# Stick-breaking attention: q out of PSUM ahead of v and weights, turned weights copied ahead of the second sigmoids

## What is computed

```python
def block(args):
    i, q_i = args
    q_pos = i * Q_BLOCK + jnp.arange(Q_BLOCK)          # Q_BLOCK = 128
    z = jnp.einsum('bhqd,bhkd->bhqk', q_i, k).astype(jnp.float32) * scale
    mask = key_pos[None, :] < q_pos[:, None]
    log_beta = jax.nn.log_sigmoid(z)
    log_one_minus = jnp.where(mask, jax.nn.log_sigmoid(-z), 0.0)
    later = lax.cumsum(log_one_minus, axis=3, reverse=True) - log_one_minus
    weights = jnp.where(mask, jnp.exp(log_beta + later), 0.0)
    return jnp.einsum('bhqk,bhkd->bhqd', weights.astype(v.dtype), v)
```

## Time and profile before

| | |
|---|---|
| median of 3 runs | 1345.59 us (1342.94 to 1350.71) |
| the profiled execution | 1345.15 us, span 1343.6 us |
| TensorE busy | 1222.4 us, 91% of the span |
| VectorE busy | 902.5 us, 67% |
| ScalarE busy | 741.0 us, 55% |
| GpSimd busy | 305.6 us, 23% |

### The profile page before, as it was taken

One profiled execution on the slowest core, in us unless ns is written; L12 is line 12 of the kernel. 1 busy time (PEld: TensorE's weight loads), 2 busy tenths in 40 slices (PEclk: granted clock), 3 DMA queues, 4 the chain that ended last, 5 costly groups with the idle time before them and its releaser, 6 DMA issues. The chain is left out here.

```text
span 1343.6 us, 18137 instructions
## 1 busy us (share of the span) xinstructions
PE 1222.4 (91%) x6596; PEld 957.9 (71%) x6596; DVE 902.5 (67%) x847; ACT 741.0 (55%) x758; POOL 305.6 (23%) x270
## 2 busy tenths in 40 slices
PE   3999999999899988599937999999999999999975
PEld 2778776877688767388825777777777777777742
DVE  4256565655466258334576989898898888988825
ACT  6155555554352233312234787777777877777713
POOL 0000000000211001000051444444444444444400
PEclk9999999999899995599967999999999999999988
DMA  5210101000211020173328999999999999999747
GB/s 172 63 32 17 32 17 31 18 17 1 64 32 32 1 94 32 45 244 109 111 97 292 408 387 383 382 382 386 384 384 375 381 377 385 374 391 389 293 175 296
DMA packets 85840, 271.63 MB, mean 202 GB/s; under 512 B 14640, under 2 KB 48544, under 8 KB 61216
## 3 DMA queue, kind: packets, MB, share of 16 engines
q1 hardware_dynamic: 75760, 249.89, 50.2%
q0 software_dynamic: 8880, 16.87, 3.8%
q10 hardware_dynamic: 1152, 4.19, 0.8%
HBM read 253.91 MB, written 25.79 MB: 208 GB/s over the span
## 5 line engine op out<-in xcount | busy, mean ns | idle before, releaser
L1886 PE MATMUL ps<-w_high,x_hi 128*128 128x512 f32 x512 | 206.3, 403 | 4.8 <-DVE hid L1812 2.9
L1886 PE MATMUL ps<-w_lower,x_hi 128*128 128x512 f32 x512 | 203.5, 397 | 0.0
L1886 PE MATMUL ps<-w_high,x_lo 128*128 128x512 f32 x512 | 203.4, 397 | 0.0
L1153 POOL DMA_INDIRECT x_g<-h_dram,who x33 | 160.2, 4854 | 40.2 <-POOL who L1149 27.6
L1826 DVE TENSOR_TENSOR d_lo<-cat,d_hi 128x2048 fp32r<-128x2048 f32 x64 | 146.3, 2287 | 25.5 <-ACT d_hi L1747 25.5
L1798 DVE TENSOR_TENSOR w_lower<-w_raw,w_high 128x2048 fp32r<-128x2048 f32 x62 | 141.7, 2286 | 24.7 <-ACT w_high L1726 24.7
L1803 DVE TENSOR_TENSOR w_lower<-w_raw,w_high 128x2048 fp32r<-128x2048 f32 x64 | 143.4, 2279 | 0.0
L1732 ACT ACTIVATE w_high<-w_raw 128x2048 fp32r<-128x2048 f32 x62 | 118.8, 1917 | 25.5 <-PE ps L1886 25.5
L1747 ACT ACTIVATE d_hi<-cat 128x2048 fp32r<-128x2048 f32 x64 | 122.2, 1910 | 17.0 <-PEq L1233 13.5
L1726 ACT ACTIVATE w_high<-w_raw 128x2048 fp32r<-128x2048 f32 x62 | 118.3, 1908 | 0.0
L1886 PEld LDWEIGHTS ps<-w_high,x_hi 128*128 128x128 f32 x512 | 97.0, 189 | 28.5 <-DVE w_lower L1798 3.3
(11 more groups left out here) (276 smaller groups left out, 2401.0 us busy)
## 6 DMA issues: line engine op xcount, KB each, us to landing
w_raw<-exp_w_gate SPq DMA_DIRECT2D x64, 1024.0 KB, 7.0
w_raw<-exp_w_up SPq DMA_DIRECT2D x64, 1024.0 KB, 9.0
cat<-exp_w_down SPq DMA_DIRECT2D x64, 1024.0 KB, 8.0
w_raw<-w_in SPq DMA_DIRECT2D x25, 512.0 KB, 3.9
xt<-x SPq DMA_DIRECT2D x8, 512.0 KB, 7.6
w_raw<-w_out SPq DMA_DIRECT2D x8, 512.0 KB, 5.3
x_g<-x SPq DMA_DIRECT2D x8, 512.0 KB, 3.8
x_dram<-cat SPq DMA_DIRECT2D x8, 512.0 KB, 4.9
```

The source lines that it names most:

```text
L1153: pool.indirect_dma_start(x_g[0:CAP, j, :], None, k["h2_dram"][:, :], bass.IndirectOffsetOnAxis(ap=who[j][0:CAP, 0:1], axis=0), bounds_che ...
L1886: mm = pe.matmul(out, x_[:, n // 3, :], w_[:, n // 3, :], start=(n == 0), stop=(n == 3 * KD - 1))
```

## The change

It has two parts. In step 0 of each pair, `evict` and `evict_lo` of the group that ends there (q's first half) stand ahead of `copy_v` and the split, on ScalarE and on VectorE; in all other steps they stay where they were. And `sigmoids` is cut in two, `scan_sigmoids` and `weight_sigmoids`: in steps 3 to 6 of each pair `copy_w(g-1)` stands between the two, in the other steps behind both, as before. Nothing is added or left out: each engine has as many instructions as before.

```diff
+    copies_first = (3, 4, 5, 6)
...
-            def sigmoids(g):
+            def scan_sigmoids(g):
                 b = g % 2
                 if g >= 2:
                     act.wait_ge(scan_done, 2 * g - 2)
...
                     act.activation(stay[:, b, :, s:e], ps[:, 2 * (c % 2):2 * (c % 2) + 2, 0:e - s], ACT.Sigmoid,
                                    scale=-SCALE).then_inc(stay_done, 1)
+
+            def weight_sigmoids(g):
+                b = g % 2
                 if g >= 2:
                     act.wait_ge(turned, turns[g - 2] + len(parts(g - 2)))
                 for n, (s, e) in enumerate(chunks(g)):
...
                 if g < STEPS:
-                    sigmoids(g)
+                    scan_sigmoids(g)
+                    if n not in copies_first:
+                        weight_sigmoids(g)
                 if g >= 1:
                     copy_w(g - 1)
+                if g < STEPS and n in copies_first:
+                    weight_sigmoids(g)
+                ends = p < SB_PAIRS and 24 in (part[1] for part in fill[n] if part)
+                if ends and n == 0:
+                    evict(6 * (p + 1) + group_at[n])
                 if g < STEPS and n == 0:
                     copy_v(p)
                 if g < STEPS and n in split_at and 3 * p + split_at[n] < TILES:
                     split_hi(3 * p + split_at[n])
-                if p < SB_PAIRS and 24 in (part[1] for part in fill[n] if part):
+                if ends and n:
                     evict(6 * (p + 1) + group_at[n])
...
                 if g < STEPS:
                     weights(g)
-                    if n in split_at and 3 * p + split_at[n] < TILES:
-                        split_lo(3 * p + split_at[n])
-                if p + 1 < SB_PAIRS and group_at[n] < 4 and 24 in (part[1] for part in fill[n] if part):
+                lows_out = p + 1 < SB_PAIRS and group_at[n] < 4 and 24 in (part[1] for part in fill[n] if part)
+                if lows_out and n == 0:
+                    evict_lo(6 * (p + 1) + group_at[n])
+                if g < STEPS and n in split_at and 3 * p + split_at[n] < TILES:
+                    split_lo(3 * p + split_at[n])
+                if lows_out and n:
                     evict_lo(6 * (p + 1) + group_at[n])
                 if g >= 1:
                     evict_o(g - 1)
```

## The result

The changed kernel takes 1332.83 us (median of 4 runs, 1331.71 to 1333.32), the kernel before 1344.41 us (median of 4, 1342.94 to 1350.71; a fourth run of 1343.23 us joined the three shown ahead of the prediction). The ratio is 0.9906 with a 95% interval of 0.9877 to 0.9935: faster by 0.9%, clear of no change. Forecast were 1336.7 us, with a range of 1332 to 1342, and a gain of 8.5; the median moved by 11.6, and the time lies at the low end of the range. The profiled executions differ by about as much: span 1343.6 before, 1331.5 now.

What follows compares the result with a forecast made beforehand. TensorE, busy 91% of the span, was taken as the bound, so only its waits and slow clock could be won. The terms -9.4 + 2.1 - 1.2 = -8.5 us took 1345.15 to 1336.7 us, range 1332 to 1342.

Steps and rivals of the forecast that it cites:

- The bound and the mechanism of q: TensorE, 91% busy, bounds; early q removes step 1's three 1.91 us waits for `q_lo` and the slow clock behind.
- -9.4: Step 1 of all pairs: 6.2 us of waits and 3.2 us of slow clock in pairs 1 and 2 go.
- The copies in the first three pairs: Steps 3 to 6: late second sigmoids delay `k_lo`, costing 0.7 us a pair, +2.1 us in all.
- The copies in the last pair: Steps 3 and 4: nothing waits for low parts, so gaps of 0.89 and 0.31 us are won, -1.2 us.
- All later work follows it unchanged, so this goes to the end: Behind the stage: its closing barrier passes the summed gain of 8.5 us unchanged to the end of the run.
- One: Step 4: the new 1.3 us wait for `k_lo` pulls the clock down, 1338.3 to 1341.5 us; chance 0.26.
- Two: Step 1: the clock's falls stay or come back later, hanging on something besides the gap, 1339.9 us; chance 0.13.
- Three: First three pairs: `k_lo` doesn't bind, so the copies win 0.89 us each, 1331.9 us; chance 0.08.
- Four: Steps 3 and 5: ScalarE reloads its table when switching between copy and sigmoid, +15.4 us, 1352.1 us; chance 0.03.
- the bound of 1338.9: Whole run: a time under it, a change of 0.5% or 6.7 us, counts as faster.

Runs made afterwards that it cites:

- experiment 1: The changed kernel with only q let out first in step 0, no copies moved: 1331.62 us, ratio 0.9899.
- experiment 6: The kernel before the change, with ScalarE splitting the weight tile of step 0 twice for a longer gap: 1357.38 us, ratio 1.0065.
- Experiment 2: The changed kernel with only the copies moved, q back behind the copies of v and the split: 1342.20 us, ratio 0.9979.
- experiment 3: The changed kernel with copies first in steps 3 and 4 only, no longer in 5 and 6: 1333.15 us, ratio 0.9906.
- experiment 4: The changed kernel with copies first in the last pair only: 1331.82 us, ratio 0.9883.
- experiment 5: The kernel of experiment 3, with VectorE making `k_lo` ahead of the multiplication in step 3: 1333.22 us, ratio 0.9887.

## Why the prediction was right or wrong

**The bound and the mechanism of q** were right. The wait for `q_lo` and the slow clock behind it are both gone in all pairs; experiment 1 has the whole gain of the stage from this part alone, and experiment 6 shows that a longer gap brings half clock in every pair. The term "-9.4" was mis-sized: it measured -10.4 (9.94 + 11.53 + 11.57 + 8.49 less 31.12). Its clock part, 3.2 us, came as forecast; the waits gave 7.2 instead of 6.2. I took the gap as the profile's idle time, 1.91 us. That is counted from the modelled end of the turning, and a matmul that follows at once starts before that end (at 143.48, where the turning ends at 143.10 + 0.63 = 143.73). From start to start the place shrank by 2.53 - 0.38 = 2.15 us, 0.24 more than the idle time, and about as much more in each of the four pairs.

**The copies in the first three pairs** were right to 0.2 us. Forecast: a wait of 1.3 us for `k_lo` in step 4, 0.5 in step 6, 0.7 us lost a pair. Measured: 1.48, 0.53 and 0.65. Experiment 2 gives the same with q last, in experiment 3 the wait and the loss of step 6 go alone, in experiment 4 both waits, and 5 shows which order on VectorE makes the wait.

**The copies in the last pair** were mis-sized the same way: -1.2 from the idle times, -1.8 measured, 1.64 of it in steps 3 and 4, where the records say 0.89 and 0.31 and the starts 1.10 and 0.54. The two parts together: +2.1 - 1.2 forecast, +0.2 measured.

**"All later work follows it unchanged, so this goes to the end"** is the step that failed for the whole run. It put what happens behind the stage at nothing, and the runs showed 1.3 us of gain there in the median (11.6 less 10.25) and 1.8 in the span. Of the 3.1 us by which the gain exceeded the forecast, this is the largest part; 1.0 lie in "-9.4" and 0.7 in the two terms of the copies. (Another 0.7 us of the distance between 1336.7 and 1332.83 is the base, since I counted from 1345.15 and the median before is now 1344.41.) Behind the stage the time depends on where the granted clock falls and rises; the prediction kept a chance of 0.08 for that and no term. Part of it is chance: two profiles of the same kernel differ by 0.8 us there, and those of all kernels but experiment 6's by 4.7. But the medians moved by 11.6 us in both sets of runs of the changed kernel, 1.3 to 1.4 beyond the stage each time, and the 1.4 us of the last eight matmuls stand in every profile of the changed kernel and its edits. The intervals of the ratios are 6 to 8 us wide, so whether the gain behind the stage is the change's doing isn't shown, and its cause stays open.

**The rivals.** One (the new wait pulls the clock down): not seen in any of the twelve waits of 1.5 us in four profiles. Two (the falls stay): excluded by experiments 1 and 6, as in the six profiles without the gaps the clock doesn't fall between the start of the stage and the last step of the last pair, and longer gaps brought more falls. The Trainium skill, page "TensorE: Matmul & The Clock Gate", section on HAM oscillation, ties a fall of the clock to an idle gap longer than any of these. The traces disagree, with falls at gaps of 1.53, 1.91 and 3.00 us. Three (`k_lo` doesn't bind): excluded by 2 and 4. Four (table loads): the stage has a single load in the changed kernel too, at 70.43, and the sigmoids follow the copies at once, at 161.88 in pair 1.

**A slip beside the chances.** The prediction says that its forecast leaves 1.8 us to the bound of 1338.9; that holds for 1337.1. From the 1336.7 that it names it is 2.2.

## What to carry to other kernels

When an engine program is written by hand, ask of each result who waits for it and put it ahead of work that nobody asks for yet: here one eviction and one subtraction moved into idle time made all of the stage's gain, and the matching move of the copies made none, because the chain through VectorE to `k_lo` set the step. Removing a wait pays only up to the next engine's chain, so follow the chain from the same start on the other engines before counting it. Judge a change of under 1% by the stage's own length in the trace, from start to start, when the rest of the run moves by several us of itself. A difference in that rest that stands in several profiles may still belong to the change, so look at where the profiles part before calling it chance.

The best order found is experiment 5's: q first, copies first in steps 3 and 4, and `k_lo` ahead of the multiplication in step 3. Its stage is 14.0 us shorter than before and 3.8 than the changed kernel's; whole runs taken together are 1333.22 and 1335.98 us for it and the changed kernel, and the intervals of their ratios overlap. Experiments 3 and 4 lie 1.9 and 1.5 us under the changed kernel in the stage, but their whole-run intervals overlap its.

## What the runs showed of the hardware

- Short gaps of TensorE can cost their length again. A gap of 1.91 us brought half clock in two of three cases, in both kernels that had it; one of 3.00 us in three of three, one of 1.53 us in the one case there was. In these eight cases the clock fell between 0.9 us ahead of the gap's end and 1.2 us behind it. Each fall cost 1.4 to 1.6 us over the 24 matmuls of 512 columns that follow, and 2.8 in pair 0 of experiment 6 (13.83 us less the 9.94 of before and the 1.09 that the gap grew).
- The length of the gap doesn't decide it alone: the twelve gaps of 1.5 us ahead of step 4's projection brought no fall, the one of 1.53 in step 1 did. And of the three gaps of 1.91 us one brought none, in both kernels. What stands ahead of the gap differs: in step 1 eight transposes of v, one set of score matmuls and four transposes of weights, in step 4 the products with v and two sets of score matmuls. Which of this matters wasn't tried.
- The idle time ahead of a matmul understates what removing it gives: 1.91 us of idle were 2.15 from start to start (pair 1, step 1).
- The end of a run can hold a difference of its own: the same last eight matmuls took 6.6 us in two profiles and 5.1 to 5.4 in seven, by when the clock came back.
